# A block-triangular inverse on TensorE that computes and moves only the columns that can be non-zero

## What is computed

```python
def frame_step(S, inp):
    r_t, w_t, k_t, v_t, kk_t, a_t = inp
    sa = jnp.einsum('bhvk,bhk->bhv', S, -kk_t)
    S = (S * w_t[:, :, None, :]
         + sa[..., None] * (kk_t * a_t)[:, :, None, :]
         + v_t[..., None] * k_t[:, :, None, :])
    o_t = jnp.einsum('bhvk,bhk->bhv', S, r_t)
    return S, o_t
```

## Time and profile before

| what | value |
|---|---|
| median of 3 runs | 2743.78 us (2743.17 to 2747.65) |
| the profiled execution's own time | 2744.07 us |
| its span, first to last instruction | 2742.2 us |
| mean granted TensorE clock | 0.978 |
| TensorE matmuls busy | 2553.0 us, 93% of the span |
| VectorE busy | 1395.3 us, 51% |
| ScalarE busy | 910.6 us, 33% |
| GpSimd busy | 1147.4 us, 42% |

### The profile page before, as it was taken

One profiled execution on the slowest core, in us unless ns is written; L12 is line 12 of the kernel. 1 busy time (PEld: TensorE's weight loads), 2 busy tenths in 40 slices (PEclk: granted clock), 3 DMA queues, 4 the chain that ended last, 5 costly groups with the idle time before them and its releaser, 6 DMA issues.

```text
span 2742.2 us, 46926 instructions
## 1 busy us (share of the span) xinstructions
PE 2553.0 (93%) x18466; PEld 2077.3 (76%) x18466; DVE 1395.3 (51%) x1997; ACT 910.6 (33%) x1444; POOL 1147.4 (42%) x657
## 2 busy tenths in 40 slices
PE   6798899999899998999996999999999988999998
PEld 4575688887787877888875888887887766788886
DVE  3624873345513258454277566666659963321122
ACT  3233422223523334222254333333333334332231
POOL 3433544444444435444454333333333325444442
PEclk8999999999999999999998999999999999999999
DMA  5310223232221112323322111111112222233331
GB/s 152 80 54 16 85 92 100 92 100 85 77 93 35 58 62 85 99 92 94 98 71 73 41 33 41 41 33 33 33 57 87 89 62 83 87 99 98 94 100 54
DMA packets 56465, 202.67 MB, mean 74 GB/s; under 512 B 6768, under 2 KB 7448, under 8 KB 56304
## 3 DMA queue, kind: packets, MB, share of 16 engines
q1 hardware_dynamic: 54144, 195.84, 22.5%
q0 software_dynamic: 1328, 3.68, 0.8%
q10 hardware_dynamic: 832, 0.82, 0.1%
HBM read 196.64 MB, written 3.67 MB: 73 GB/s over the span
## 4 chain that ended last, share of the span: by engine, by line
PE 78%; DVE 11%; issue 4%; ACT 4%; POOL 2%; DMA 0%; DVEq 0%; SPq 0%; ACTq 0%; POOLq 0%
PE banks L1800 21%; PE banks L1801 21%; PE banks L1802 21%; PE banks L2244 8%; ACT sb_pa L635 1%; PE banks L2285 1%; DVE banks L1592 1%; PE banks L2018 1%; DVE sb_zr L1502 1%; POOL sb_pa L1678 1%; PE banks L1980 1%; DVE sb_x L1078 1%; PE banks L2144 1%; PE banks L1933 1%; PE banks L2001 1%
## 5 line engine op out<-in xcount | busy, mean ns | idle before, releaser
L1652 POOL TENSOR_TENSOR sb_wl<-sb_raw,sb_wh 128x1024 fp32r<-128x1024 f32 x365 | 897.3, 2460 | 1235.9 <-ACT sb_wh L454 1235.7
L1800 PE MATMUL banks<-sb_bh,sb_wh 128*128 128x512 f32 x2656 | 1061.8, 400 | 93.9 <-POOL sb_bl L1664 28.0
L1801 PE MATMUL banks<-sb_bl,sb_wh 128*128 128x512 f32 x2656 | 1047.1, 394 | 0.0
L1802 PE MATMUL banks<-sb_bh,sb_wl 128*128 128x512 f32 x2656 | 1045.9, 394 | 0.0
L1800 PEld LDWEIGHTS banks<-sb_bh,sb_wh 128*128 128x128 f32 x2656 | 505.4, 190 | 227.4 <-issue 53.9
L1802 PEld LDWEIGHTS banks<-sb_bh,sb_wl 128*128 128x128 f32 x2656 | 505.1, 190 | 110.5
L1801 PEld LDWEIGHTS banks<-sb_bl,sb_wh 128*128 128x128 f32 x2656 | 505.8, 190 | 107.4 <-issue 2.2
L454 ACT CAST sb_wh<-sb_raw 128x1024 fp32r<-128x1024 f32 x365 | 381.4, 1046 | 542.6 <-PE banks L1802 538.0
L2244 PE MATMUL banks<-sb_m 64*64 64x64 f32 (+1 forms) x5632 | 205.7, 228 | 8.4 <-DVE sb_m L1542 7.6
L2244 PEld LDWEIGHTS banks<-sb_m 64*64 64x64 f32 x5632 | 195.7, 134 | 20.1 <-issue 12.4
L998 DVE SCALAR_TENSOR_TENSOR sb_x<-sb_x,banks 128x512 f32 x72 | 49.5, 688 | 315.0 <-PE banks L1802 315.0
(11 more groups left out here) (319 smaller groups left out, 2628.0 us busy)
## 6 DMA issues: line engine op xcount, KB each, us to landing
sb_raw<-w SPq DMA_DIRECT2D x365, 512.0 KB, 3.5
sb_x<-xT SPq DMA_DIRECT2D x4, 512.0 KB, 6.6
out<-sb_x SPq DMA_DIRECT2D x4, 512.0 KB, 2.7
bias_rows<-sb_brow POOLq DMA_DIRECT2D x1, 1536.0 KB, 35.1
sb_bias<-bias_rows POOLq DMA_DIRECT2D x1, 1024.0 KB, 6.7
sb_pj<-pT POOLq DMA_DIRECT2D x2, 512.0 KB, 3.9
sb_wm<-wm ACTq DMA_DIRECT2D x1, 288.0 KB, 3.4
sb_rope<-rope ACTq DMA_DIRECT2D x1, 256.0 KB, 3.0
```

The source lines that it names most:

```text
L1652: nc.gpsimd.tensor_tensor(wl[:, s, :], raw[:, s, :], wh[:, s, :].bitcast(F32), ALU.subtract).then_inc(lo_ready, 1)
L1800: nc.tensor.matmul(out, hi_a, hi_b, start=first, stop=False)
L1801: nc.tensor.matmul(out, hi_a, lo_b, start=False, stop=False)
L1802: return nc.tensor.matmul(out, lo_a, hi_b, start=False, stop=last)
```

## The change

The columns of the 64x64 matrices that a level can change are half of all: the chunk's columns fall in pieces of b, and `z` and `t` are non-zero only in the even pieces, `x` only in the odd ones. `half_of(m, b, s)` is the view of these columns (32 of 64, in runs of b), `packed(product, b)` the view of 32 adjacent columns in the bank. Now

- the moving operand of `z` (levels 4 to 32), `t` (2 to 16) and `x` (2 to 32) holds 32 columns in place of 64; the stationary operand is the whole 64x64 matrix as before, and so are number and order of the matmuls and their waits;
- ScalarE's copy of z4, z8, z16 and z32 moves 128x128 elements in place of 128x256; z2 is copied whole;
- VectorE's addition of `t` and `x` works on 128x128 in place of 128x256. For `x` it is a SCALAR_TENSOR_TENSOR that multiplies the product by a 0/1 value of the row (`even_rows`, one [P, 1] column of `wm` for each level) before it adds, since the rows of `M_Z`'s columns that are not copied give rows that must not be added;
- the mask tile `wm` grows by one matrix of 64 columns.

```diff
+        def half_of(m, b, s):
+            kept = m.rearrange("p c (a s b) -> p c a s b", s=2, b=b)
+            return kept[:, :, :, s, :]
+
+        def packed(product, b):
+            return bank(product)[:, :, 0:32].rearrange("p c (a b) -> p c a b", b=b)
...
+                def move_kept(b):
+                    for g in range(2):
+                        st.wait(half_pe, n, f"z{b}.{g}")
+                        st.did(half_act, f"z{b}.{g}", nc.scalar.copy(half_of(one(g, M_Z), b, 0), packed(f"z{b}.{g}", b)))
...
-                move("z4", M_Z)
+                move_kept(4)
...
-                    for m, dst in (("t", M_T), ("x", M_X)):
-                        if m + str(b) != "t32":
-                            grouped(f"{m}{b}", lambda g: did(f"{m}{b}.{g}", V.tensor_tensor(
-                                one(g, dst), one(g, dst), bank(f"{m}{b}.{g}"), ALU.add)))
+                    if b != LEVELS[-1]:
+                        grouped(f"t{b}", lambda g: did(f"t{b}.{g}", V.tensor_tensor(
+                            half_of(one(g, M_T), b, 0), half_of(one(g, M_T), b, 0), packed(f"t{b}.{g}", b), ALU.add)))
+                    even_rows = wm[:, 9, LEVELS.index(b):LEVELS.index(b) + 1]
+                    grouped(f"x{b}", lambda g: did(f"x{b}.{g}", V.scalar_tensor_tensor(
+                        half_of(one(g, M_X), b, 1), packed(f"x{b}.{g}", b), even_rows, half_of(one(g, M_X), b, 1),
+                        ALU.mult, ALU.add)))
...
+                                        if kept:
+                                            level, side = kept
+                                            rhs = half_of(m_all[r, b, 4 * g + j:4 * g + j + 1, :], level, side)[:, 0]
+                                            last = nc.tensor.matmul(packed(f"{name}.{g}", level)[r, j], lhs, rhs, start=True, stop=True,
+                                                                    skip_group_check=True)
+                                            continue
...
-                    product(f"z{b}", [(M_OFF, M_T)], needs=[by_pool(f"off{b}"), by_dve(last_t)])
+                    product(f"z{b}", [(M_OFF, M_T)], needs=[by_pool(f"off{b}"), by_dve(last_t)], kept=(b, 0) if b > 2 else None)
...
-                        product(f"t{b}", [(M_X, M_Z)], needs=[by_act(f"z{b}"), by_dve(last_x)])
-                    product(f"x{b}", [(M_Z, M_X)], needs=[by_act(f"z{b}"), by_dve(last_x)])
+                        product(f"t{b}", [(M_X, M_Z)], needs=[by_act(f"z{b}"), by_dve(last_x)], kept=(b, 0))
+                    product(f"x{b}", [(M_Z, M_X)], needs=[by_act(f"z{b}"), by_dve(last_x)], kept=(b, 1))
```

More of the change, by code:

```diff
@@ L233, in build @@
             m_s = sb("m_s", [P, 9, 64], F32, part)
-            wm = sb("wm", [P, 9, 64], F32, part)
+            wm = sb("wm", [P, 10, 64], F32, part)
             eye = sb("eye", [P, 64], F32, part)
@@ L904, in half @@
                 last = n == NC - 1
-                move("z4", M_Z)
+                move_kept(4)
                 if not last:
                     decay_tanh(n + 1)
-                move("z8", M_Z)
+                move_kept(8)
                 if not last:
                     rate_tanh(n + 1)
-                move("z16", M_Z)
+                move_kept(16)
                 split(Idx(0, p0 + 4 * n + 6))
-                move("z32", M_Z)
+                move_kept(32)
                 move("tt", (M_TA, M_TW))
@@ L2214, in waits, with product @@
                             pe.wait_ge(sema, before(sema, n) + max(of))
-                def product(name, *outs, needs=()):
+                def product(name, *outs, needs=(), kept=None):
                     for g in range(2):
@@ L2464, in layout @@
     wm += [(i // (2 * b) == j // (2 * b)) & (i // b < j // b) for b in (2, 4, 8, 16, 32)]
+    wm += [np.concatenate([i // b % 2 == 0 for b in (2, 4, 8, 16, 32)] + [i < 0] * 59, axis=1)]
     A["wm"] = np.stack(wm, axis=1).astype(np.float32)
```

## The result

The changed kernel takes 2750.14 us (median of 20 runs, 2744.93 to 2757.85) against 2744.12 us (20 runs, 2741.09 to 2747.65): 1.0024 times as long, interval [1.0017, 1.0030]. It is 6.0 us slower; 2739.8 was forecast, with 2746 as the upper end. The profiled execution took 2750.46 us, span 2748.6, at a mean granted clock of 0.972 (before 2744.07, 2742.2 and 0.978).

A forecast was written before the change was run, and what follows sets the result against it. The inverse was taken as bound by TensorE up to the z16 product and then by the scan, which waits for GpSimd. 7 x 0.47 + 0.63 = 3.9 us gave 2739.8 us, range 2733 to 2746.

The forecast's parts named there:

- The load as TensorE's limit: In the inverse's products, loading 64 stationary columns sets the step: an estimated 56 ns against 59 for an instruction pair.
- the faster step: Rival, inverse's matmuls: TensorE's step falls with fewer moving columns, down to 2717 us; chance 0.17 for over 6 us gained.
- the slower one from a strided operand: Rival, every kept product from t2 on: moving runs of 2 to 32 words feed the array more slowly, 2766 us; chance 0.08.
- the prediction's rival: Step falls in the inverse's matmuls; a 60-cycle floor would give 50 ns a pair, 13 us gained, 2731; chance 0.17.
- The copies and additions: ScalarE's z4 to z32 copies fall to 0.27 us, VectorE's additions to 287 ns (t) and 344 ns (x).
- nothing is gained: Rival: short runs slow ScalarE's copies, or x additions with a pointer wait for GpSimd; 2744 to 2745 us, chance 0.13.
- the stall: Between z.1 and t.0 of a level, TensorE waits for z.0's copy; t.0 can start 0.133 us earlier, within 0.17.
- the shorter matmul: In each level's products, a matmul with 32 fewer moving columns ends 26 ns earlier after its last start.
- The sum: 0.47 us in each of pairs one to seven up to the scan's end, 0.63 in the eighth; 3.9 us in all.
- from 59 ns (nothing): Bound taken for an instruction pair's step in the inverse's matmuls: it stays at 59 ns; the other bound was 29.6.
- its signs: Profile after: copy 0.27 us, level 2.88, additions 0.29 and 0.34, scan 1.1 behind L1652, pairs but the last 0.47 shorter.
- follow each other: Behind the inverse, `tt`, the 8 steps and the next pair's first products run in the chain, taking none of the gain back.

The follow-up runs named there:

- e8: Changed kernel with only 8 moving columns in every kept product, so the inverse is another one; 2794.63 us beside 2744.44.
- e9: Changed kernel with 32 stationary columns as well, leaving out half the rows of every kept product; 2733.83 us beside 2744.78.
- e1: Changed kernel with 64 moving columns again, halved copies and additions kept; 2741.51 us, ratio 0.9986 to the kernel before.
- e3: Changed kernel with VectorE's scan moved from behind level 16 to behind the x32 additions; 2733.97 us, ratio 0.9959 to the kernel before.
- e6: Changed kernel with 64 moving columns in x32 alone; 2739.73 us, ratio 0.9989 to the kernel before.
- e7: Changed kernel with 24 added 64x64 matmuls between x32 and tt in the first seven pairs; 2741.59 us, ratio 0.9994 to the kernel before.
- e2: Changed kernel with z4 to z32 copies at full size again, each packed column copied twice; 2749.74 us, ratio 1.0013 to the kernel before.

## Why the prediction was wrong

**What held.** The load as TensorE's limit, and with it the step of 29.6 ns: 467 ns a group at 8, 32 and 64 columns (e8, after, before), 254 with half the stationary columns (e9). So the faster step didn't come (chance 0.17); nor did the slower one from a strided operand (0.08). The Trainium skill ("TensorE: Matmul & The Clock Gate", LDWEIGHTS) puts a load at columns/1.2 ns, 53 ns for 64 and 27 for 32 by an estimate from it; two instructions, one of each head, took 58 and 32 ns here, both some 5 ns above it. The Trainium skill also has an overhead of some 60 cycles a matmul ("TensorEngine Tiling (Array Packing)", Instruction Overhead), by an estimate 25 ns at 2.4 GHz. Read as the spacing of instructions, as the prediction's rival read it, it doesn't hold for these tiles: e9's instructions start every 15.9 ns, over both heads.

**The copies and additions.** 0.27, 0.287 and 0.344 us were forecast, 0.266, 0.289 and 0.351 measured; neither short runs nor the pointer scalar brought a penalty, so the rival "nothing is gained" fell. A level went from 3.02 to 2.88 us as forecast. Of its 0.133, the stall from z.1's last start to t.0's first gave 0.107 (224 to 117 ns). The other 0.027 is the shorter matmul, but at another place than was costed. Inside a run of products the latency is 219 ns at 32 columns and 218 at 64, so z.1 doesn't end earlier. Only the first product behind a stall is shorter, 240 ns in place of 267, and the starts behind it come 27 ns earlier: its group of starts spans 436 ns, and 463 before. That the size came out as costed (0.026) while the place did not is partly luck.

**The sum.** 0.47 us a pair was right to 0.01 in the pairs that kept the clock (62.83 against 63.30), and the scan still set their end:

```profile
1750.00 2.35 POOL L1668 TENSOR_TENSOR sb_wl<-sb_raw,sb_wh 128x1024 fp32r<-128x1024 f32 x1 [0.26 <-ACT sb_wh L462]
```

```profile
1750.93 2.49 DVE L1449 TENSOR_TENSOR_SCAN sb_w<-sb_going,sb_t 128x512 f32<-128x512 f32 x1
```

It ends at 1753.42, 1.07 us behind GpSimd's 1752.35, as in the earlier trace rows. Over all, 3.9 us were forecast; e1, which has these edits with the old operand, gained 3.3 by the medians and 3.8 by its ratio (0.0014 of 2744.81).

**The step that failed** is the first of the change's parts, "number, order, waits and weight loads (64 columns each) stay; the moving columns halve", with its price "from 59 ns (nothing)". It asked only whether thinner products could be faster, or slower by a stride, and gave the granted clock no term. Nearly all of its signs came out (copy, level, additions, scan); that every pair but the last gets shorter did not, and none of them looks at the clock. What the runs showed in its place: the moving columns under the load's limit cost next to no time, but what TensorE streams also bears on its clock. With half of it, the wait of 1.1 to 1.5 us ahead of `tt` goes with 1.2 GHz in five pairs of seven. 3.4 us at that level made a pair 1.6 to 2.1 us longer than the shortest, and 6.8 us in the first pair 2.9. `tt` and `mp`, which the prediction had "follow each other" unchanged, pay it: their matmuls take 417 ns in place of 269. e1 takes the loss away from the side of the operand, e3 from the side of the wait, e6 and e7 with a little more streaming at the wait. The Trainium skill ("TensorE: Matmul & The Clock Gate", HAM oscillation — how this bites in real kernels) tells of the clock falling at waits between short bursts of matmuls. This case agrees in part: here the clock falls at a wait too, but the wait is no new one, only the work beside it grew thinner, and with 8 moving columns it falls without a wait (e8).

**Open.** Which pairs lose the clock changes from pair to pair and run to run (after spans 2744.93 to 2757.85 us, e3 2732.68 to 2735.35), and no run here shows what decides it. In the profiled execution the span is 6.4 us longer: 5.5 in the seven pairs, 3.1 ahead of them and 2.2 less behind them. The 3.1 come with more time at 0.50 in stages that the change doesn't touch (99 us ahead of the recurrence, 89 before). e1's profile shows as much low clock there, and the first pair begins anywhere from 1526.9 (e8) to 1533.1 us (e2) with the same code ahead of it, so that is not the thin operand's. That the pairs' 5.5 us and the medians' 6.0 lie so close is therefore in part chance.

## What to carry to other kernels

Where the weight load sets TensorE's step, halving the moving columns gains next to no time, and beside a wait of a microsecond or so it can cost the clock: look at the granted clock where the next full-width products run, not at PE's busy share. Keep the moving operand wide, take the halves out of the bank with the copies and additions, which is where the gain was (e1), and take the wait away if its cause can be moved (e3: one line, 11 us). If a wait must stay, a little streaming in it can keep the clock (e7).

## What the runs showed of the hardware

- Back-to-back weight loads did not keep TensorE's clock: with 8 moving columns it fell to 0.50 and stayed there for 17.1 or 20.5 us (e8).
- A 64x64 product's latency stayed at 218 to 219 ns when its moving columns went from 64 to 32, and was 199 at 8. Only behind a stall did it show the columns: 267 ns for 64 and 240 for 32.
- VectorE's scan over two SBUF tensors takes 1216 ns by itself and 2.4 to 2.5 us beside GpSimd's subtraction, while the additions with a bank, one SBUF tensor and a pointer scalar never took over 352 ns.
- With 64x32 tiles two instructions go in 32 ns; then "issue" becomes TensorE's longest wait (21.7 of the 27.4 us that it waits ahead of these products, e9).
